# A mixture-of-experts layer on one core: scatter-add of expert outputs replaced by old rows gathered and added on VectorE, with routing computed while the output projection runs

## The reference

```python
scores = sigmoid(h @ w_router); sel = scores + router_bias
# the sum of the two best of each group of 8 experts ranks the 8 groups; experts of the best 4 remain
_, eidx = top_k(where(emask, sel, -inf), 6)          # 6 of 64 experts per token
wts = scores[eidx] / sum * 2.5
# the (token, expert) pairs sorted by expert, each expert padded to whole blocks of 128 slots
yb = swiglu(x_pad[tok_buf], w_gate[e], w_up[e], w_down[e])      # per block of one expert
y  = zeros.at[tok_buf].add(yb * w_buf)
x  = x + gt_f * rmsnorm(y + swiglu(h, shared weights), gain)
```

## Time and profile before

| what | value |
|---|---|
| runs | 1505.17 us median, 1498.16 to 1523.48 |
| the profiled execution: its time, its span | 1506.51 us, 1504.7 us |
| busy, share of the span | PE 91%, PE weight load 61%, DVE 61%, ACT 42%, POOL 29% |
| DMA | 351 MB, 233 GB/s over the span; q1 (SP) 279 MB, q0 (POOL) 71 MB |
| longest groups | DVE remainders L487 288 us, PE down product L1727 311 us, PE three passes L1624 to L1626 some 790 us |
| POOL L786 (the adds) | 83, 9.9 us from issue to landing (median) |
| POOL L778 (the gathers) | 86, 8.2 us |

### The profile page before, as it was taken

The page is one execution under the profiler, slowest core; times in us unless marked ns, Lnnn a source line. Parts: engine busy times, 40 slices in busy tenths (PEclk is TensorE's granted clock), DMA queues, the critical chain, the costliest instruction groups (busy, mean ns, idle before and its releaser), DMA issues.

```text
span 1504.7 us, 26347 instructions
## 1 busy us (share of the span) xinstructions
PE 1375.3 (91%) x6360; PEld 916.8 (61%) x6361; DVE 916.2 (61%) x1493; ACT 633.3 (42%) x885; POOL 437.5 (29%) x252
## 2 busy tenths in 40 slices
PE   5899998899997987999999999999999999999950
PEld 1467654545556765776677667766676676776630
DVE  0746676912226854877667775686766557677626
ACT  1510006722224233655545554555554346455513
POOL 2000000013445522433433333334334333333323
PEclk9999998999998988999999999999999999999975
DMA  8935414032215136999999999999999888999966
GB/s 301 333 102 171 145 28 116 1 154 101 107 65 197 56 113 216 322 317 312 360 290 318 341 322 349 276 291 330 349 308 323 215 233 262 313 318 320 289 138 237
DMA packets 104887, 351.27 MB, mean 233 GB/s; under 512 B 14691, under 2 KB 16839, under 8 KB 104564
## 3 DMA queue, kind: packets, MB, share of 16 engines
q1 hardware_dynamic: 79864, 279.39, 51.2%
q0 software_dynamic: 24704, 71.27, 20.9%
q10 hardware_dynamic: 284, 0.16, 0.1%
HBM read 307.02 MB, written 62.19 MB: 245 GB/s over the span
## 4 chain that ended last, share of the span: by engine, by line
PE 55%; DMA 28%; SPq 5%; issue 4%; DVE 4%; ACT 3%; POOL 1%; ACTq 0%; POOLq 0%; DVEq 0%
DMA raw<-in_w_up_dram 16%; PE ps L1727 10%; DMA y_acc<-arena,idxs 9%; PE ps L1594 8%; PE ps L1503 7%; PE ps L1624 7%; PE ps L1625 6%; PE ps L1626 6%; PE ps L1706 2%; SPq L577 2%; SPq L537 1%; PE ps L1508 1%; DMA arena<-in_w_ada_dram 1%; PE ps L1478 1%; DMA arena<-in_x_prompt_dram 1%
## 5 line engine op out<-in xcount | busy, mean ns | idle before, releaser
L487 DVE TENSOR_TENSOR lo_ring<-raw,hi_gate_up (+1 forms) x128 | 287.6, 2289 | 81.6 <-ACT hi_gate_up L961 58.4
L1727 PE MATMUL ps<-raw,aT 128*128 x664 | 310.6, 611 | 10.6 <-ACT aT L1029 8.8
L786 POOL DMA_INDIRECT y_acc<-arena,idxs x83 | 169.3, 2039 | 397.4 <-DMA y_acc<-arena,idxs 272.4
L961 ACT ACTIVATE hi_gate_up<-raw (+1 forms) x128 | 237.9, 1906 | 104.7 <-SPq L655 70.1
L1624 PE MATMUL ps<-hi_gate_up,xTh 128*128 x664 | 268.5, 404 | 3.3 <-DVE xTl L1365 3.2
L1626 PE MATMUL ps<-hi_gate_up,xTl 128*128 x664 | 261.4, 394 | 0.0
L1625 PE MATMUL ps<-lo_ring,xTh 128*128 x664 | 261.3, 394 | 0.0
L778 POOL DMA_INDIRECT arena<-h_rows,idxg x86 | 154.4, 1795 | 194.4 <-DVE idxg L1348 168.4
L1727 PEld LDWEIGHTS ps<-raw,aT 128*128 128x128 f32 x664 | 121.2, 192 | 133.6 <-issue 133.5
L1624 PEld LDWEIGHTS ps<-hi_gate_up,xTh 128*128 128x128 f32 x664 | 125.8, 189 | 28.5 <-issue 4.3
L1365 DVE TENSOR_TENSOR xTl<-ps,xTh 128x1024 fp32r<-128x1024 f32 x84 | 102.7, 1223 | 65.1 <-ACT xTh L1021 65.1
(11 more groups left out here) (249 smaller groups left out, 1557.0 us busy)
## 6 DMA issues: line engine op xcount, KB each, us to landing
raw<-in_w_gate_dram SPq DMA_DIRECT2D x128, 512.0 KB, 5.9
raw<-in_w_up_dram SPq DMA_DIRECT2D x128, 512.0 KB, 9.1
raw<-in_w_down_dram SPq DMA_DIRECT2D x64, 1024.0 KB, 11.2
arena<-in_w_ada_dram SPq DMA_DIRECT2D x32, 512.0 KB, 6.3
arena<-in_w_ada_dram SPq DMA_DIRECT2D x4, 2048.0 KB, 20.1
arena<-in_x_prompt_dram SPq DMA_DIRECT2D x16, 512.0 KB, 9.0
x_rows<-arena SPq DMA_DIRECT2D x8, 512.0 KB, 2.8
h_rows<-arena SPq DMA_DIRECT2D x8, 512.0 KB, 2.6
```

Source lines behind the costliest of these rows:

```text
L487: return eng.tensor_tensor(lo_of(e, m), raw_of(e, m), hi_of(e, m).bitcast(F32), ALU.subtract)
L786: pool.indirect_dma_start(out=y_acc, out_offset=bass.IndirectOffsetOnAxis(ap=idxs[b][:, 0:1], axis=0), in_=yw[b], in_offset=None, bounds_c ...
L961: act.activation(hi_of(e, m), raw_of(e, m), ACT.Copy).then_inc(round_gu, 1)
L1727: ins = pe.matmul(bank(2 + half), aT[:, k, :], down[:, k, 512 * half:512 * half + 512], start=(k == 0), stop=(k == KF - 1))
```

## The change

Expert outputs are no longer accumulated by DMA. `old_rows(i)` gathers the tile's present sums from DRAM into yw, `y_of` on DVE (instead of ACT) computes PSUM x weight + yw, and `new_rows(i)` stores the rows back with a plain indirect DMA. Padding slots are skipped by the bounds check, and so read and write nothing. There are two accumulators in DRAM, one for even and one for odd tiles: y_acc0 starts with the shared expert's output, y_acc1 with zeros that POOL stores early. `slot_columns(i)`, which fetches the tile's weights and indices for old_rows and y_of, waits on DVE until the store of tile i-2 has landed. In the tail SP loads both, and DVE adds them.

Routing is done tile by tile within mixing: `sigmoid(t-2)` on ACT, `route_a(t-2)` and `route_b(t-3)` on DVE, `logits` and `rank` on PE between the halves of `mix(t)`. Each (token, expert) pair gets its slot number there; from mixing tile 4 on POOL writes pairs of token number and weight to a table in DRAM with six indirect DMAs a tile, three before each of its two additions, and the rest after mixing. Once all have landed, one indirect DMA fetches each tile's 128 slots as a row (`blocks`), PE transposes it, and the loop finds indices and weights in tables; one_hot and slots are gone from the loop. Work of the shared expert moves from POOL to DVE. x_t uses other PSUM banks, so the loop's first steps no longer wait for the shared expert's last. Weights of experts 2 and 3 are requested at the end of the shared expert instead of after the first gathers.

The diff, cut to its core:

```diff
@@ SP
+                if t == NT - 2:
+                    sp.wait_ge(shg_mm, NT)
+                    load_gate_up(0, 2)
                 sp.wait_ge(shy_s, t + 1)
...
-            for b in range(2):
-                sp.wait_ge(gathered[b], 16)
-            load_expert(0, 2)
             load_expert(0, 3)
...
-            sp.wait_ge(added, 16 * (last + 3))
+            sp.wait_ge(added[1], ((last + 1) & 126) * 8 + ADDED_0[1])
             for t in range(NT):
+                sp.dma_start(z_t(t)[0:ROWS[t], :], y_acc[1][P * t:P * t + ROWS[t], :]).then_inc(x_in[t], 16)
+            sp.wait_ge(added[0], (last & 126) * 8 + 16)
+            for t in range(NT):
+                sp.dma_start(y_t(t)[0:ROWS[t], :], y_acc[0][P * t:P * t + ROWS[t], :]).then_inc(x_in[t], 16)
@@ POOL
+            pool.dma_start(slot_rows.rearrange("(e r) c -> e (r c)", e=NE), tr[0:NE, 0:2 * CAP]).then_inc(tab_init, 16)
...
+            for t in range(NT):
+                pool.dma_start(y_acc[1][P * t:P * t + ROWS[t], :], zero[0:ROWS[t], :]).then_inc(added[1], 16)
+            def scatter_slots(t, k0, k1):
+                r = slice(0, ROWS[t])
+                for k in range(k0, k1):
+                    pool.indirect_dma_start(out=slot_rows, in_=pairs[r, t, k, :], in_offset=None,
+                                            out_offset=bass.IndirectOffsetOnAxis(ap=dest[r, t, k:k + 1], axis=0),
+                                            bounds_check=slot_bound, oob_is_err=False).then_inc(tab_st, 16)
...
+                if t >= LAG:
+                    pool.wait_ge(slots_s, t - LAG + 1)
+                    scatter_slots(t - LAG, 0, TOPK // 2)
...
-            def scatter_add(i, b):
-                pool.wait_ge(added, 16 * (i + 2))
+            def old_rows(i, b):
+                pool.wait_ge(slot_col, i + 1)
+                pool.sem_inc(pool_turn, 1)
+                pool.indirect_dma_start(out=yw[b], out_offset=None, in_=y_acc[b],
+                                        in_offset=bass.IndirectOffsetOnAxis(ap=idxs[b][:, 0:1], axis=0),
+                                        bounds_check=gather_bound, oob_is_err=False).then_inc(y_old[b], 16)
+            def new_rows(i, b):
                 pool.wait_ge(yw_s, i + 2)
...
             def tile(i, odd):
                 pool.wait_ge(xt_mm, i + 2)
                 gather(i + AHEAD, 1 - odd)
-                scatter_add(i - 1, 1 - odd)
+                old_rows(i, odd)
+                new_rows(i - 1, 1 - odd)
@@ ACT, in tile
-                y_of(i - 1, 1 - odd)
@@ DVE
+            dve.wait_ge(tab_init, 16)
+            dve.memset(maskb[:, :, :], 0.0)
...
+            def slot_columns(i, b, first=False):
+                if not first:
+                    dve.wait_ge(added[b], 8 * (i - b) + ADDED_0[b])
...
+            def y_of(i, b):
+                dve.wait_ge(y_old[b], 8 * (i - b) + 16)
+                dve.wait_ge(dn_mm, i + 1)
+                dve.scalar_tensor_tensor(yw[b], pair(2), wcol[b][:, 0:1], yw[b], ALU.mult, ALU.add).then_inc(yw_s, 1)
...
             def tile(i, odd):
                 act_of(i)
                 xt_rest(i + 1)
-                e = dve.value_load(etab[0:1, bass.ds(i + AHEAD + 1, 1)], min_val=0, max_val=NE - 1)
-                slots(i + AHEAD, 1 - odd)
-                dve.wait_ge(added, 16 * i)
-                slot_columns(i - 1, 1 - odd)
-                one_hot(i + AHEAD + 1, e)
+                gather_column(i + AHEAD, 1 - odd)
+                slot_columns(i, odd)
+                y_of(i - 1, 1 - odd)
                 rests(i)
@@ PE, in the shared expert and in tile
+                if t == 5:
+                    pe.wait_ge(slots_s, NT + 1)
...
+                if t == 6:
+                    pe.wait_ge(tabr_in, 16)
...
-                slots(i + AHEAD, e_next)
```

More of the change, by code:

```diff
@@ new lines, in tables_b, with tables_c, mat_rest @@
+            def tables_b():
+                dve.wait_ge(route_mm, NT + 2)
+                dve.tensor_copy(tabi[:, :], bank(5)[0:1, P:3 * P]).then_inc(tables, 1)
+            def tables_c():
+                dve.wait_ge(route_mm, NT + 3)
+                link(dve.tensor_copy(itab, bank(4)[:, 0:P]))
+                link(dve.tensor_copy(wtab, bank(4)[:, P:2 * P]))
+                for b in range(2):
+                    dve.tensor_copy(idxg[b][:, 0:1], itab[:, b:b + 1]).then_inc(idx_s, 1)
+            def mat_rest(e, m):
+                dve.wait_ge(round_gu, 2 * e + m + 1)
+                split_rest(dve, e, m).then_inc(lo_gu, 1)
@@ L1382, in _ @@
             xt_rest(1)
[L1383 to L1386 removed]
+            gather_column(2, 0)
+            gather_column(3, 1)
+            slot_columns(0, 0, first=True)
             last = dve.value_load(lasti[0:1, NE - 1:NE], min_val=NE - 1, max_val=MAX_TILES - 1)
@@ L1592, in mix @@
                 for half in range(2):
+                    if half == 1:
+                        between()
                     for k in range(KD):
@@ L1612, in logits, with rank, between @@
                 ins.then_inc(log_mm, 1)
-            for t in range(NT):
-                mix(t)
+            def rank(t):
+                pe.wait_ge(maskb_s, min(t + 1, NT))
+                if 1 <= t < 8:
+                    pe.wait_ge(slots_s, t)
+                elif t >= 8:
+                    pe.wait_ge(h2t_s, NT)
+                out = rank_at(t)
+                for s in range(min(t + 1, NT)):
+                    ins = pe.matmul(out, (triub if s == t else onesb)[:, :], maskb[:, s, :],
+                                    start=(s == 0), stop=(s == min(t, NT - 1)))
+                ins.then_inc(route_mm, 1)
+            for t in range(NT):
+                def between():
+                    if t >= 2:
+                        logits(t - 2)
+                    if t >= 3:
+                        rank(t - 3)
+                mix(t, between)
                 if t >= 1:
                     h2_t(t - 1)
-                if t >= 2:
-                    logits(t - 2)
-            logits(NT - 2)
             def passes(out, at_h, at_l, w_h, w_l, k, first, last):
@@ L1690, in expert @@
             def expert(i):
                 return pe.value_load(etab[0:1, bass.ds(i, 1)], min_val=0, max_val=NE - 1)
-            def slots(i, e=None, first=False):
-                e = expert(i) if e is None else e
-                if not first:
-                    pe.wait_ge(idx_s, i)
-                pe.wait_ge(oh_s, i + 1)
-                for t in range(NT):
-                    ins = pe.matmul(bank(6)[:, 0:5], oh[:, t, :], wp[:, t, bass.ds(e, 1), :].rearrange("p a c -> p (a c)"),
-                                    start=(t == 0), stop=(t == NT - 1))
-                ins.then_inc(slot_mm, 1)
```

612 lines of the change are left out of this document (316 added, 296 removed).

## The result

The changed kernel takes 1563.98 us (median of 4 runs, 1558.03 to 1571.93), the kernel before on the same chip 1502.01; the ratio is 1.0428, with a 95% interval of 1.0373 to 1.0482. The forecast was 1470. The rival "the chain of stores sets it" had said 1567.

A forecast was written before the change was run, and what follows sets the result against it. PE was taken to bound the loop, with DMA close behind; 1506.5 + 1 + 3 - 28 - 15 + 3 = 1470.5, so 1470 us. The forecast's own range was 1452 to 1495, the overall range 1436 to 1545.

The forecast's parts named there:

- the chain of stores sets it: Loop rival: stores land as late as the gathers, 8.3 us, giving a period of 11.6 and 1567 us; chance 0.19.
- First 306 us: Before mixing: more zero stores and the slot table on POOL's queue cost +1 us, bounds 0 and +6.
- Mixing, +3: 306 to 447 us: POOL's additions and six slot scatters take 16.6 against 16.39 us; +3 with ranks, bounds +1 and +30.
- slot scatters are dear: Mixing rival: a scatter takes 2.6 us, POOL needs 20.8 against 16.4 and the table comes late; 1517 us, chance 0.13.
- doesn't take the routing off the path: Mixing and shared expert rival: DVE's routing ends after the matmuls, 2 us longer per mixing tile, 3 per shared; 1508, chance 0.10.
- Shared expert and lead-in, -28: 447.6 to 577.6 us: 92 us of PE work plus 10 of waiting for the table, 102 instead of 130; bounds -38 and 0.
- The loop, -15: Tile loop: 82 periods of 10.35 us plus 5 for weights, 854 us, so -15; bounds -36 and +82.
- The period is the larger of 10.09 and L + 3.4: Tile loop: PE's 10.09 us or a store's landing time plus 3.4 for copies, POOL's start and old_rows sets each tile.
- I take 7.3 where DMA is full and 5.7 elsewhere: Tile loop: assumed landing of a plain indirect store in us, giving periods of 10.7 and 10.09.
- the first sign of being wrong: Tile loop: distances between act_t exceed 11 us with DMA at 0.9 or less.
- The third: End of lead-in: the forecast is wrong if act_t(0) comes after 570 us.
- The tail, +3: After act_t(82): last store lands some 6 us sooner, extra loads and sums cost 9 to 11; +3, bounds -5 and +12.

The follow-up runs named there:

- stores alone: Kernel with scatter-adds of valid rows into one accumulator, but each scatter is a plain store and nothing is fetched: 1437.85 us.
- the remainders ahead: Changed kernel with the weight remainders on VectorE moved ahead of slot_columns and y_of: 1541.27 us.
- the two kernels of 4.: Changed kernel with VectorE's weight remainders held back until the store is issued, 1532.88 us, or moved ahead of slot_columns and y_of, 1541.27 us.
- the two kernels with adds: Changed kernel's routing with scatter-adds into one accumulator instead of fetch, sum and store: valid rows only 1466.16 us, all 128 rows 1470.04 us.
- the one with two accumulators: Kernel with scatter-adds of valid rows, but adds alternate between two accumulators and the tail sums both: 1482.47 us.
- held-back remainders: Changed kernel with VectorE's weight remainders held back until GpSimd has issued the store: 1532.88 us.
- 7.: Mixing test: kernel with scatter-adds of valid rows, route_b's product and sum over ranks done three times, 1467.35 us; also shows timelines of the changed kernel.
- two-tile chain: Changed kernel with a separate index column for the fetch, no VectorE wait for stores, and store i-1 issued ahead of old rows i: 1659.89 us.

## Why the prediction was wrong

- *First 306 us*: right (+1.1).
- *Mixing, +3*: +10.5; at 151.3 us the stage is past the 150 that I had named as a sign of being wrong. I had looked at GpSimd's 5.2 + 6 x 1.9 us; a slot scatter takes 0.97 and 0.30 between two, so GpSimd had room (and the rival "slot scatters are dear" was nowhere near). The failing part is VectorE: 6 to 7 us of routing were to lie beside the matmuls. route_a alone takes 9, in the piece of the tile in which the next root waits for VectorE, and in three tiles a shared weight's remainder stands ahead of it, which I had not seen. So a part of the rival "doesn't take the routing off the path" came true in the mixing, with half of what it had there (10.5 against 3 + 18).
- *Shared expert and lead-in, -28*: -23.2, close, but partly by luck: PE took 70 us to the table's transposes, where I had 60 (508 less 447.6), and then stood for 3.12 us and not for some 10. act_t(0) came at 566.1 here and at 559.5 to 563.7 in the other executions with the same first part, before 577.6; the forecast 553 missed by the mixing and some 5 us. In the changed kernel's chain stands a y store of the shared expert that landed after 19.67 us, issued right behind the first experts' 6 MB on SP's queue.
- *The loop, -15*: +60.4, the step that failed. "The period is the larger of 10.09 and L + 3.4" has the right ring, and the wait named in advance is the one that is there. "I take 7.3 where DMA is full and 5.7 elsewhere" is the mis-sized term: L measured 8.8 in the median, and between 680 and 760 us 11.0 for the stores with a long issue and some 10 over all seven; in the light stretch it was 6.2. A store issued in 1.0 us does land near 7.3 where DMA is full (7.6 with stores alone, 7.5 with the remainders ahead); the change puts it at the side of the remainders on VectorE, which stretches its issue to 3.0 in half of the tiles. I had priced the issue like a gather's (1.85, within its landing of 8.3), though my own sentence on the wait named the remainders as standing right behind y_of, that is, beside the store. The link was smaller than mine, 2.4 instead of 3.4. The chain's rival (L 8.2, 1567) was right in place and nearly in size, and I had given it 0.19 against 0.38, because I read "a slower loop empties the DMA queues" as a bound on L: the queues were at 0.87 instead of 0.99, and L was above the 8.3 of the gathers all the same. The distances of 13.6 at 0.87 are the first sign of being wrong that I had named. The third, act_t(0) after 570, did not come (566.1).
- What the term also left out: even with L at my 7.3 (the two kernels of 4.), the loop was 899 to 902, not 854. The period is a mean over tiles of which some land after 10 or 11 us, and what one tile loses is not won back by the next, since no tile takes less than PE's 10.0: a median under the limit is not enough. By an estimate from the 83 landings with the remainders ahead, each tile taken as the larger of 10.0 and L + 2.4, the spread gives 873 of the 899; the other 26 us are other waits, of which the 109.5 us that VectorE waits for ScalarE's rounding, now ahead of y_of, is the likeliest, though no run shows it.
- *The tail, +3*: +9.5, within my bound of +12. The second accumulator's loads and sums cost 12 to 15 (the two kernels with adds against the one with two accumulators); that the last store lands sooner gave less than the 6 us I had counted: it took 8.60 us from its issue to its landing.
- The Trainium skill (DMA: Bandwidth & Descriptors, Anatomy of one DMA) was cited against my value for L, with a store landing no sooner than a gather. In these runs the traces agree with it: with stores alone the gathers of the same rows landed after 6.8 in the median and the stores after 7.5, and in the change the fetches after 6.5 and the stores after 8.8. The rule was nearer than my inference from the plain 512 KB stores.

## What to carry to other kernels

Replacing a read-modify-write in the DMA by fetch, add and store on the engines puts a second landing, a sum and two queue hops into a ring that had one landing; alternating two accumulators only helps if no in-order queue (here VectorE's copies, then GpSimd's own order) ties the two together again. Before pricing such a ring, write down every instruction between one landing and the next issue with its queue, and take the spread of the landing, not its median. If a change has two parts, time them apart: here everything but the new accumulation, with the old adds, is 2.5% faster than before (1470.04; 0.9752, interval 0.9665 to 0.9840), and with adds of valid rows it takes 1466.16, both ahead of either kernel.

## What was not expected of the hardware

- *An indirect DMA's issue on GpSimd is held up by VectorE's subtraction of two SBUF tensors.* In the changed kernel the store's issue takes 3.06 us in the median of the 59 stores beside L499 (two pieces of 2.25 us), and 1.0 in 21 of the other 24; 3.07 is one piece and the 1.0 of the issue. It hangs on which starts first: with held-back remainders, 49 stores beside which the subtraction started 0.3 us later kept a median issue of 1.02, and 13 that it preceded took 2.25. The Trainium skill (SBUF — State Buffer, Who interferes with whom) has such instructions contend with a GpSimd instruction that reads SBUF, but reports that such an instruction did not stall a DMA in a probe, and infers that descriptor generation doesn't need the port in question; the rows here disagree for indirect DMAs (the indirect issue also reads its index column from SBUF; which of its accesses is held up, no run here shows).
- *The reverse too:* L1261, 8 elements a partition, takes 0.17 us in the tiles in which GpSimd adds nothing beside it and 2.29 at 420.76, ending at 423.05 with GpSimd's L772 (420.64 + 2.38). L1295 ends in the same way with L764. By the same page (Summary: rules for kernel authors) the later of the two waits for the whole of the other; the rows agree, those of L1345 and L1257 in 7. too.
- *Small scatters are cheap:* 54 scatters of 8 bytes a row were issued in 0.97 us each in the median (0.90 to 2.00), and GpSimd waited for the last to land for 2.16 us after its issue.
- *Not settled:* why the stores of the two-tile chain land after 5.7 us in the median, though issued in 3.06 as well, and why in the changed kernel some stores with an issue of 3.1 land after 5.4 to 5.8 and others mostly after 9 to 11.6. The loop of the two-tile chain is slower and the DMA engines emptier (0.71 to 0.79 by stretches of 200 us); whether that is the reason wasn't tried.
